# Attention scores in ten full banks instead of twelve partly filled ones

## The chip, the cores and the metric

One NeuronCore of a Trainium2 chip runs the whole kernel as one program. The metric is the device time of an execution in microseconds (us), the median of several. The engines are named as in the profile: PE is TensorE (PEld its weight loads), DVE is VectorE, ACT is ScalarE, POOL is GpSimd, and SP the queue that issues the loads. Each works through its own list of instructions strictly in the order of the program and waits at semaphores for the others.

## What is computed

One decoder layer on 512 tokens of width 1024, batch 1: a half-weighted SwiGLU, a mixer, a second half-weighted SwiGLU and a final RMS norm, each on a normalised input. The mixer projects the tokens once and has two head groups: four heads of gated linear attention (GLA) and eight heads of dilated attention, whose outputs are joined and projected by `w_out`. The part at issue is the dilated attention:

```python
q = rope_partial(aq...) * (ATT_HD ** -0.5)      # 8 heads of 64, rotary on the first 16 dims
k = rope_partial(ak...)
# for (window, dilation) in ((128, 1), (512, 4), (2048, 16)):
s = where(causal and in the window and on the stride, q @ k^T, -inf)
p = exp(s - max(s)); den = sum(p)
o = (p @ v) / den;  lse = max(s) + log(den)
# the three branches are mixed with softmax over their lse
o_att = rms_norm(sum(softmax(lse) * o), att_out_norm)
```

The kernel computes the three branches as one causal softmax with a mask in `const` that adds the log of the number of branches in which a key is seen.

## The kernel before

**Precision.** A weight product is made of three matmuls on rounded pairs (`product`, lines 1260 to 1262: high by high, high by low, low by high). So ACT rounds each weight unit from `raw` into `w_hi` (line 480, `split`) and DVE subtracts it into `w_lo` (line 776); PE waits for the count `w_split`. The matmuls of attention itself (lines 1566, 1582 and 1599) are full float32, each of those of 1566 and 1599 recorded as two instructions.

**Pairs, tiles, strips.** The eight heads are four pairs p; a pair fills the 128 partitions, with its heads e = 0 and 1 in the lower and upper 64. For a query tile i of 128 tokens the causal keys are 128(i+1) wide: a *strip* of 128, 256, 384 or 512 columns. A step s of the attention loop handles some strips of both heads in the banks `ps[4]` (e = 0) and `ps[5]` (e = 1), at most 512 columns each. Before, `ATT_TILES = ((0, 1), (2,), (3,))` gives each pair three steps of 384, 384 and 512 columns, so there are 12 steps.

**The stages of a step s**, each on its engine at loop index k:

- PE `scores(s)` at k = s (line 1566). The first step of a pair waits for `rope_done` of 2p+2 (query and key tile of the pair rotated), every step for `s_masked` of the step before.
- DVE `mask_scores(s)` at k = s (line 962): masks out of the bank into `probs` and takes the row maximum, one instruction for each strip and head.
- ACT `exp_scores(s)` at k = s (line 653): one exponential for each strip and head, with the row sum.
- DVE `scale_probs(s)` at k = s+1 (lines 984 and 991): reciprocal of the sums, then the scaling. In odd steps below `SHARED_FROM` ACT does both heads of the scaling (`scale_scalar`, line 672), from `SHARED_FROM` on ACT does e = 1 and DVE e = 0.
- PE `transpose_probs(s)` at k = s+2 (line 1582) into the banks 2 and 3, which ACT's `move_probsT(s)` copies out at k = s+2 (line 682).
- PE `weigh_values(s)` at k = s+3 (line 1599) adds to the bank 6 or 7 of the pair.

**What lies between.** PE fills each step with other work: first the projection of the remaining query and key tiles (`project_heads(n, w, half)`, half a tile of 12 products, at the indices `HEAD_STEPS`; two halves of the tile (1, 0) stand ahead of the loop), then the GLA part of the output projection (`gla_part(m, half)`, 6 products, at `PART_STEPS`). A projected tile is copied by ACT (`move_tile`, line 629, at `TILE_STEPS`) and rotated: DVE `rotate(n)` shuffles and multiplies by the sine (lines 942 and 945), POOL multiplies by the cosine (line 472), DVE `rotated(n)` adds the two (line 951) and counts `rope_done`. DVE also has `gla_gated_output` (line 1063) at k below 3, `low_concat` (line 1069), and the splits of weight units: `split_next(U + 10)` and `split_next(U + 11)` at k = 1 and 4. The unit U + 14 is split in quarters (`round_quarter` on ACT, line 662, k = 7 to 10; `split_quarter` on DVE, line 974, k = 8 to 11); only its last quarter raises `w_split`. When a pair is finished, ACT `high_heads(p)` (lines 690 and 691) and DVE `low_heads(p)` (line 997) take it out of its bank.

The order on PE in a step is this:

```python
for k in range(ATT_STEPS + 3):
    if k < ATT_STEPS:
        scores(k)
    # project_heads where HEAD_STEPS has k, gla_part where PART_STEPS has k
    if 2 <= k < ATT_STEPS + 2:
        transpose_probs(k - 2)
    if k >= 3:
        weigh_values(k - 3)
```

Of the kernel before, what the change touches and what calls it, by code (L numbers as in the profile page):

```python
# [32 lines left out]
P = 128  # L33
# [38 lines left out]
ATT_TILES = ((0, 1), (2,), (3,))  # L72
PER_PAIR = len(ATT_TILES)
ATT_STEPS = PER_PAIR * ATT_H // 2
# [3 lines left out]
SHARED_FROM = 8  # L78
# [3 lines left out]
TILE_STEPS = (0, 1, 2, 4, 5, 7)  # L82
HEAD_STEPS = (0, 0, 1, 1, 2, 3, 4, 4, 5, 6)
PART_STEPS = (7, 8, 10, 11, 12, 13, 13, 14)
# [6 lines left out]
def layer_program(nc, xw_dram, positions, gains_in, up1, down1, w_proj, w_ga, w_v, w_a2, w_o, up2, down2,  # L91
                  const_in, final_gain, out):
    ctx = ExitStack()
    with ctx:
# [67 lines left out]
        negm = sb("negm", [P, 4 * ATT_H], F32, mix)  # L162
        den = sb("den", [P, 4 * ATT_H], F32, mix)
        rden = sb("rden", [P, 4 * ATT_H], F32, mix)
# [184 lines left out]
        def strips(s):  # L349

            out, at = [], 0
            for i in ATT_TILES[s % PER_PAIR]:
                out.append((i, slice(at, at + P * (i + 1))))
                at += P * (i + 1)
            return out

        def strip_width(s):
            return strips(s)[-1][1].stop

        def stat(s, i, e):  # L360
            return 2 * (ST * (s // PER_PAIR) + i) + e

# [113 lines left out]
        def _(act):  # L476
# [170 lines left out]
            def exp_scores(s):  # L647
                for e in range(2):
                    act.wait_ge(s_masked, 2 * s + e + 1)
                    for i, cols in strips(s):  # L650
                        q = stat(s, i, e)
                        strip = probs[s % PROB_BUFS][e][:, cols]
                        ins = nc.scalar.activation(strip, strip, ACT.Exp, bias=negm[:, q:q + 1], scale=-1.0,
                                                   accum_out=den[:, q:q + 1])
                    ins.then_inc(exp_done, 1)
# [9 lines left out]
            def scale_scalar(s):  # L665
                act.wait_ge(rden_done, s + 1)
                for e in range(2):
                    if on_scalar(s, e):
                        for i, cols in strips(s):
                            q = stat(s, i, e)  # L670
                            strip = probs[s % PROB_BUFS][e][:, cols]
                            ins = nc.scalar.activation(strip, strip, ACT.Copy, scale=rden[:, q:q + 1])
                        ins.then_inc(act_scaled, 1)
# [14 lines left out]
            def high_heads(p):  # L688
                act.wait_ge(pv_done, PER_PAIR * (p + 1))
# [6 lines left out]
            for k in range(ATT_STEPS + 2):  # L696
                if k in TILE_STEPS:
                    tile = 2 + TILE_STEPS.index(k)
                    move_tile(tile // 2, tile % 2)
                if k == 8:  # L700
                    scale_scalar(k - 1)
                    move_probsT(k - 2)
                if k < ATT_STEPS:
                    exp_scores(k)
                if 1 <= k <= ATT_STEPS and k != 8 and on_scalar(k - 1, 1):
                    scale_scalar(k - 1)
                if k >= 2 and k != 8:
                    move_probsT(k - 2)
                if k in (1, 4):
                    n = (1, 4).index(k) + 1  # L710
                    split_next(U + 9 + n, 0, T + 19 + 2 * n)
                if 7 <= k < 11:
                    round_quarter(U + 14, k - 7, T + 25)
                if 1 <= k <= GLA_H:
                    high_concat(k - 1)
                if k in (7, 10, 12):
                    high_heads((7, 10, 12).index(k))
# [54 lines left out]
        def _(dve):  # L772
# [181 lines left out]
            def mask_scores(s):  # L954
                for e in range(2):
# [3 lines left out]
                    for i, cols in strips(s):  # L959
                        q = stat(s, i, e)  # L960
# [18 lines left out]
            def scale_probs(s):  # L979

                tiles = ATT_TILES[s % PER_PAIR]
                pair = slice(stat(s, tiles[0], 0), stat(s, tiles[-1], 1) + 1)
# [3 lines left out]
                for e in range(2):  # L986
                    if not on_scalar(s, e):
                        for i, cols in strips(s):
                            q = stat(s, i, e)
# [193 lines left out]
            for k in range(ATT_STEPS + 1):  # L1183
                rotates = k in TILE_STEPS
                if k == 8:
                    scale_probs(k - 1)
                if k < ATT_STEPS:
                    mask_scores(k)
                if k in (6, 8):
                    rotated(k - 1 if k == 8 else 6)  # L1190
                if k and k != 8:
                    scale_probs(k - 1)
                if rotates:
                    rotate(2 + TILE_STEPS.index(k))
                if k < 3:
                    gla_gated_output(k + 1)
                if rotates and k < 5:
                    rotated(2 + TILE_STEPS.index(k))
# [3 lines left out]
                if k in (1, 4):  # L1202
                    split_next(U + 10 + (1, 4).index(k), 0)
                if 8 <= k < 12:
                    split_quarter(U + 14, k - 8)
                if k in (8, 11, 12):
                    low_heads((8, 11, 12).index(k))
                if k == 12:
# [48 lines left out]
        def _(pe):  # L1257
# [291 lines left out]
            project_heads(1, 0, 0)  # L1549
            project_heads(1, 0, 1)  # L1550

            def scores(s):
                p = s // PER_PAIR
                if s % PER_PAIR == 0:
                    pe.wait_ge(rope_done, 2 * p + 2)
# [4 lines left out]
                for i, cols in strips(s):  # L1560
                    pieces = 2 if i else 1
                    width = P * (i + 1) // pieces
                    for c in range(pieces):
                        for e in range(2):
# [5 lines left out]
                            if i == strips(s)[-1][0] and c == pieces - 1:  # L1570
# [15 lines left out]
            def weigh_values(s):  # L1586
                p = s // PER_PAIR
                if s % PER_PAIR == 0:
# [6 lines left out]
                for i, cols in strips(s):  # L1595
# [45 lines left out]
            for k in range(ATT_STEPS + 3):  # L1641
                if k < ATT_STEPS:
                    scores(k)
                for h in range(len(HEAD_STEPS)):
                    if HEAD_STEPS[h] == k:
                        project_heads((h + 2) // 4 + 1, (h + 2) % 4 // 2, (h + 2) % 2)
# [140 lines left out]
```

## Time and profile before

| | before |
|---|---|
| median of 3 runs | 963.0 us (962.96 to 963.06) |
| the profiled execution: its own time | 962.81 us |
| its span, first to last instruction | 961.0 us |
| PE busy | 953.0 us of it |
| DVE busy, ACT busy, POOL busy | 491.4, 338.7, 52.3 us |
| granted TensorE clock, mean | 0.999 |
| attention loop on PE (first scores to the end of the last weighing) | 488.1 to 560.3 us of the span |

Times in rows are microseconds from the start of the span. In a timeline row the first number is the start and the second the duration; consecutive instructions of an engine overlap at their ends, so what an instruction costs its engine is the distance to the next start. In the chain of work that ended last, pieces stand end to end.

### The profile page before, as it was taken

The numbers are of one execution on the slowest core, as the hardware profiler recorded it, in microseconds if no ns is written. First come the engines' busy times: TensorE is split into PE (matmuls) and PEld (weight loads), VectorE is DVE, ScalarE is ACT, GpSimd is POOL, SyncE is SP. The second block draws the span as 40 slices with busy tenths as digits, with TensorE's granted clock in tenths as the row PEclk, the third lists the DMA queues.
The fourth block names the chain that finished last, engine by engine and source line by source line (L and its number), as shares of the span: only waits on it lengthen the run. The fifth ranks groups of instructions, "written<-read, shape, count | busy, mean of one in ns | idle before, by whom it ended". The sixth has DMA issues, their size and how long they took to land.

```text
span 961.0 us, 12088 instructions
## 1 busy us (share of the span) xinstructions
PE 953.0 (99%) x4714; PEld 776.2 (81%) x4714; DVE 491.4 (51%) x634; ACT 338.7 (35%) x440; POOL 52.3 (5%) x35
## 2 busy tenths in 40 slices
PE   9999999999999999999999999999999999999997
PEld 6888888888888887888778778788888888888885
DVE  6854443334443556554487768744443235644326
ACT  7323321122222334631446963433322122222313
POOL 0870000000000000000022000000000000000000
PEclk9999999999999999999999999999999999999999
DMA  8232222332221233222212012232222332255412
GB/s 324 87 132 87 76 77 92 110 127 88 91 111 55 83 102 128 88 89 88 89 44 89 29 61 87 91 129 87 87 77 87 99 131 88 90 151 152 110 44 88
DMA packets 33187, 94.76 MB, mean 99 GB/s; under 512 B 18560, under 2 KB 19840, under 8 KB 24960
## 3 DMA queue, kind: packets, MB, share of 16 engines
q1 hardware_dynamic: 16080, 91.89, 27.1%
q10 hardware_dynamic: 17072, 2.38, 1.6%
q8 instruction: 24, 0.39, 0.2%
q14 instruction: 11, 0.09, 0.0%
HBM read 90.07 MB, written 2.10 MB: 96 GB/s over the span
## 4 chain that ended last, share of the span: by engine, by line
PE 98%; DVE 1%; issue 1%; ACT 0%; DVEq 0%
PE bank L1260 31%; PE bank L1261 30%; PE bank L1262 30%; PE bank L1566 1%; PE bank L1599 1%; PE bank L1582 1%; PE bank L1378 1%; PE bank L1312 0%; PE bank L1320 0%; PE bank L1322 0%; PE bank L1277 0%; PE bank L1461 0%; DVE x_tok L1075 0%; PE bank L1498 0%; PE bank L1447 0%
## 5 line engine op out<-in xcount | busy, mean ns | idle before, releaser
L1260 PE MATMUL bank<-h_hi,w_hi 128*128 128x512 f32 x824 | 323.5, 393 | 0.0
L1262 PE MATMUL bank<-h_hi,w_lo 128*128 128x512 f32 x824 | 320.8, 389 | 0.0
L1261 PE MATMUL bank<-h_lo,w_hi 128*128 128x512 f32 x824 | 320.7, 389 | 0.0
L480 ACT ACTIVATE w_hi<-raw 128x2048 fp32r<-128x2048 f32 (+2 forms) x87 | 154.7, 1778 | 331.8 <-PE bank L1262 329.9
L776 DVE TENSOR_TENSOR w_lo<-raw,w_hi 128x2048 fp32r<-128x2048 f32 (+2 forms) x87 | 184.6, 2122 | 83.7 <-ACT w_hi L480 83.2
L1260 PEld LDWEIGHTS bank<-h_hi,w_hi 128*128 128x128 f32 x824 | 154.7, 188 | 36.4 <-issue 3.8
L1262 PEld LDWEIGHTS bank<-h_hi,w_lo 128*128 128x128 f32 x824 | 154.7, 188 | 32.3
L1261 PEld LDWEIGHTS bank<-h_lo,w_hi 128*128 128x128 f32 x824 | 154.7, 188 | 32.2 <-issue 0.7
L822 DVE TENSOR_TENSOR prod<-bank,rstd 128x512 f32<-128x512 f32 x44 | 30.4, 690 | 175.9 <-PE bank L1262 175.9
L1260 PE MATMUL bank<-g_hi,w_hi 128*128 128x512 f32 x272 | 105.8, 389 | 0.0
L1261 PE MATMUL bank<-g_lo,w_hi 128*128 128x512 f32 x272 | 105.8, 389 | 0.0
L1262 PE MATMUL bank<-g_hi,w_lo 128*128 128x512 f32 x272 | 105.8, 389 | 0.0
L521 ACT ACTIVATE gate<-gate 128x512 f32<-128x512 f32 x44 | 27.8, 632 | 158.4 <-DVE gate L820 158.3
L838 DVE SCALAR_TENSOR_TENSOR x<-bank,x 128x512 f32 (+1 forms) x24 | 16.6, 692 | 91.0 <-PE bank L1262 91.0
L1260 PEld LDWEIGHTS bank<-g_hi,w_hi 128*128 128x128 f32 x272 | 51.1, 188 | 10.6
L1261 PEld LDWEIGHTS bank<-g_lo,w_hi 128*128 128x128 f32 x272 | 51.1, 188 | 10.6
L1262 PEld LDWEIGHTS bank<-g_hi,w_lo 128*128 128x128 f32 x272 | 51.1, 188 | 10.6
L820 DVE TENSOR_TENSOR gate<-bank,rstd 128x512 f32<-128x512 f32 x44 | 30.2, 685 | 24.9 <-PE bank L1262 22.9
L472 POOL TENSOR_TENSOR projT<-projT,rope_c 128x512 f32<-128x512 f32 x8 | 13.9, 1733 | 455.0 <-DVE square L942 431.3
L831 DVE TENSOR_TENSOR g_lo<-prod,g_hi 128x512 f32 (+1 forms) x44 | 33.5, 760 | 0.7 <-ACT g_hi L525 0.7
L825 DVE TENSOR_TENSOR prod<-prod,gate 128x512 f32<-128x512 f32 x44 | 31.7, 722 | 3.2 <-ACT gate L521 0.6
L1260 PE MATMUL bank<-w_hi,g_hi 128*128 128x512 f32 x80 | 31.1, 389 | 0.0
(217 smaller groups left out, 841.5 us busy)
## 6 DMA issues: line engine op xcount, KB each, us to landing
raw<-in_up SPq DMA_DIRECT2D x43, 1024.0 KB, 4.8
raw<-in_w_proj SPq DMA_DIRECT2D x8, 1024.0 KB, 4.8
raw<-in_down1a SPq DMA_DIRECT2D x8, 768.0 KB, 4.4
raw<-in_down2a SPq DMA_DIRECT2D x8, 768.0 KB, 4.3
raw<-in_down1b SPq DMA_DIRECT2D x8, 640.0 KB, 3.8
raw<-in_down2b SPq DMA_DIRECT2D x5, 1024.0 KB, 4.9
raw<-in_w_v SPq DMA_DIRECT2D x4, 1024.0 KB, 4.8
raw<-in_w_o SPq DMA_DIRECT2D x4, 1024.0 KB, 4.8
```

Source lines behind the costliest of these rows:

```text
L472: nc.gpsimd.tensor_tensor(projT[:, t, :], projT[:, t, :], rope_c[:], ALU.mult).then_inc(rope_cos, 1)
L480: nc.scalar.activation(w_hi[u % 2][:, 0:size], raw[u % 2][:, 0:size], ACT.Copy).then_inc(w_round, 1)
L521: nc.scalar.activation(gate[:], gate[:], ACT.Silu).then_inc(silu_done, 1)
L776: nc.vector.tensor_tensor(w_lo[u % 2][:, 0:size], raw[u % 2][:, 0:size], w_hi[u % 2][:, 0:size].bitcast(F32), ALU.subtract).then_inc(w_spl ...
L820: nc.vector.tensor_tensor(gate[:], ps[bank][:], rstd[:], ALU.mult).then_inc(tile_out, 1)
L822: nc.vector.tensor_tensor(prod[:], ps[bank + 1][:], rstd[:], ALU.mult).then_inc(tile_out, 1)
L825: nc.vector.tensor_tensor(prod[:], prod[:], gate[:], ALU.mult).then_inc(g_mul, 1)
L831: nc.vector.tensor_tensor(g_lo[:, f, :], prod[:], g_hi[:, f, :].bitcast(F32), ALU.subtract).then_inc(g_ready, 1)
L838: nc.vector.scalar_tensor_tensor(x[:, m, 0:S], ps[4 + j][:], 0.5, x[:, m, 0:S], ALU.mult, ALU.add).then_inc(tile_out, 1)
L1260: nc.tensor.matmul(out, a_hi, b_hi, start=first, stop=False)
L1261: nc.tensor.matmul(out, a_hi, b_lo, start=False, stop=False)
L1262: return nc.tensor.matmul(out, a_lo, b_hi, start=False, stop=last)
```

## The change

The strips of two neighbouring pairs are packed together, so that each of ten steps has exactly 512 columns in each bank. For the pairs 0 and 1 (and again for 2 and 3) the five steps hold, as (pair, query tile): (0,0) with (0,2); (0,3); (0,1) with (1,1); (1,0) with (1,2); (1,3). The third of them holds a strip of either pair. `PAIR_BEGIN` is (0, 2, 5, 7) and `PAIR_END` (2, 4, 7, 9). The strips and their widths stay the same.

The work between the steps is placed anew: the second query/key tile of pair 1 is projected ahead of the loop (two more half tiles there, eight instead of ten in the loop), `SHARED_FROM` is 6, the split of U + 12 comes at k = 0 and that of U + 13 at k = 3, the quarters at k = 6 to 9 on ACT and 7 to 10 on DVE, and `gla_part`, `high_heads` and `low_heads` at earlier indices. The order on ACT that was special at k = 8 is gone.

```diff
 N_CONST = 1795
-ATT_TILES = ((0, 1), (2,), (3,))
-PER_PAIR = len(ATT_TILES)
-ATT_STEPS = PER_PAIR * ATT_H // 2
+ATT_TILES = tuple(tuple((base + p, i) for p, i in tiles) for base in (0, 2)
+                  for tiles in (((0, 0), (0, 2)), ((0, 3),), ((0, 1), (1, 1)), ((1, 0), (1, 2)), ((1, 3),)))
+ATT_STEPS = len(ATT_TILES)
+PAIR_BEGIN = [min(s for s in range(ATT_STEPS) if any(q == p for q, i in ATT_TILES[s])) for p in range(4)]
+PAIR_END = [max(s for s in range(ATT_STEPS) if any(q == p for q, i in ATT_TILES[s])) for p in range(4)]
 HALF = S // 2
...
 MOVES = 16
-SHARED_FROM = 8
+SHARED_FROM = 6
 NORM = {0: 0, 2: 3}
...
 ATT_BANKS = (6, 2, 3, 7)
-TILE_STEPS = (0, 1, 2, 4, 5, 7)
-HEAD_STEPS = (0, 0, 1, 1, 2, 3, 4, 4, 5, 6)
-PART_STEPS = (7, 8, 10, 11, 12, 13, 13, 14)
+TILE_STEPS = (0, 0, 1, 3, 4, 6)
+ROTATE_STEPS = (0, 1, 2, 3, 4, 6)
+HEAD_STEPS = (0, 0, 1, 2, 3, 3, 4, 5)
+PART_STEPS = (6, 7, 8, 9, 10, 11, 11, 12)
 MAGIC = 1.5 * 2.0 ** 23
...
             out, at = [], 0
-            for i in ATT_TILES[s % PER_PAIR]:
-                out.append((i, slice(at, at + P * (i + 1))))
+            for p, i in ATT_TILES[s]:
+                out.append((p, i, slice(at, at + P * (i + 1))))
                 at += P * (i + 1)
...
         def strip_width(s):
-            return strips(s)[-1][1].stop
-
-        def stat(s, i, e):
-            return 2 * (ST * (s // PER_PAIR) + i) + e
+            return strips(s)[-1][2].stop
+
+        def stat(s, p, i, e):
+
+            return 4 * s + 2 * ATT_TILES[s].index((p, i)) + e
...
             def high_heads(p):
-                act.wait_ge(pv_done, PER_PAIR * (p + 1))
+                act.wait_ge(pv_done, PAIR_END[p] + 1)
                 nc.scalar.activation(sq_att[p], ps[6 + p % 2][:], ACT.Square).then_inc(att_squared, 1)
...
             for k in range(ATT_STEPS + 2):
-                if k in TILE_STEPS:
-                    tile = 2 + TILE_STEPS.index(k)
-                    move_tile(tile // 2, tile % 2)
-                if k == 8:
-                    scale_scalar(k - 1)
-                    move_probsT(k - 2)
+                for tile in range(2, 8):
+                    if TILE_STEPS[tile - 2] == k:
+                        move_tile(tile // 2, tile % 2)
                 if k < ATT_STEPS:
                     exp_scores(k)
-                if 1 <= k <= ATT_STEPS and k != 8 and on_scalar(k - 1, 1):
+                if 1 <= k <= ATT_STEPS and on_scalar(k - 1, 1):
                     scale_scalar(k - 1)
-                if k >= 2 and k != 8:
+                if k >= 2:
                     move_probsT(k - 2)
-                if k in (1, 4):
-                    n = (1, 4).index(k) + 1
+                if k in (0, 3):
+                    n = (0, 3).index(k) + 1
                     split_next(U + 9 + n, 0, T + 19 + 2 * n)
-                if 7 <= k < 11:
-                    round_quarter(U + 14, k - 7, T + 25)
+                if 6 <= k < 10:
+                    round_quarter(U + 14, k - 6, T + 25)
                 if 1 <= k <= GLA_H:
                     high_concat(k - 1)
-                if k in (7, 10, 12):
-                    high_heads((7, 10, 12).index(k))
+                if k in (6, 8, 11):
+                    high_heads((6, 8, 11).index(k))
             nc.scalar.activation(credit[:], ones[:, 0:1], ACT.Ln)
...
             for k in range(ATT_STEPS + 1):
-                rotates = k in TILE_STEPS
-                if k == 8:
-                    scale_probs(k - 1)
                 if k < ATT_STEPS:
                     mask_scores(k)
-                if k in (6, 8):
-                    rotated(k - 1 if k == 8 else 6)
-                if k and k != 8:
+                if k == 5:
+                    rotated(6)
+                if k:
                     scale_probs(k - 1)
-                if rotates:
-                    rotate(2 + TILE_STEPS.index(k))
+                if k in ROTATE_STEPS:
+                    rotate(2 + ROTATE_STEPS.index(k))
                 if k < 3:
                     gla_gated_output(k + 1)
-                if rotates and k < 5:
-                    rotated(2 + TILE_STEPS.index(k))
+                if k in ROTATE_STEPS and k != 4:
+                    rotated(2 + ROTATE_STEPS.index(k))
                 if 2 <= k < 2 + GLA_H:
...
                     low_concat(g, cat_lo[:, g, :], o_gla[g][:], cat_hi[:, g, :])
-                if k in (1, 4):
-                    split_next(U + 10 + (1, 4).index(k), 0)
-                if 8 <= k < 12:
-                    split_quarter(U + 14, k - 8)
-                if k in (8, 11, 12):
-                    low_heads((8, 11, 12).index(k))
-                if k == 12:
+                if k in (0, 3):
+                    split_next(U + 10 + (0, 3).index(k), 0)
+                if 7 <= k < 11:
+                    split_quarter(U + 14, k - 7)
+                if k in (7, 9, 10):
+                    low_heads((7, 9, 10).index(k))
+                if k == ATT_STEPS:
                     add_heads(1)
...
             gla_spread()
-            project_heads(1, 0, 0)
-            project_heads(1, 0, 1)
+            for part_of in range(4):
+                project_heads(1, part_of // 2, part_of % 2)
             def scores(s):
-                p = s // PER_PAIR
-                if s % PER_PAIR == 0:
-                    pe.wait_ge(rope_done, 2 * p + 2)
+                if s in PAIR_BEGIN:
+                    pe.wait_ge(rope_done, 2 * PAIR_BEGIN.index(s) + 2)
                 if s:
...
                     pe.wait_ge(gla_half, 2)
-                for i, cols in strips(s):
+                for p, i, cols in strips(s):
                     pieces = 2 if i else 1
...
             def weigh_values(s):
-                p = s // PER_PAIR
-                if s % PER_PAIR == 0:
+                if s in PAIR_BEGIN:
+                    p = PAIR_BEGIN.index(s)
                     if p >= 2:
...
                 pe.wait_ge(pt_out, 2 * s + 2)
-                for i, cols in strips(s):
+                for p, i, cols in strips(s):
                     for j in range(i + 1):
...
                     if HEAD_STEPS[h] == k:
-                        project_heads((h + 2) // 4 + 1, (h + 2) % 4 // 2, (h + 2) % 2)
+                        project_heads(h // 4 + 2, h % 4 // 2, h % 2)
                 for h in range(len(PART_STEPS)):
...
                         gla_part(h // 2, h % 2)
```

## Rows read from the trace of the kernel before

**Rows 1.** The page: busy time, granted clock (tenths), chain that ended last.

```profile
PE 953.0 (99%) x4714; PEld 776.2 (81%) x4714; DVE 491.4 (51%) x634; ACT 338.7 (35%) x440; POOL 52.3 (5%) x35
...
PEclk9999999999999999999999999999999999999999
...
PE 98%; DVE 1%; issue 1%; ACT 0%; DVEq 0%
```

**Rows 2.** The chain in order of time, 486 to 566: start, us, what.

```profile
488.14 0.87 PE bank L1566 x12
489.01 0.43 PE bank L1260
...
494.67 0.85 PE bank L1566 x8
...
517.65 0.87 PE bank L1582 x8
518.52 0.81 PE bank L1599 x12
519.33 1.06 PE bank L1566 x8
...
524.02 1.02 PE bank L1599 x16
...
560.28 0.43 PE bank L1260
...
563.31 0.86 PE bank L1660 x2
```

**Rows 3.** Timeline of DVE in the attention loop.

```profile
488.29 2.29 DVE L776 TENSOR_TENSOR w_lo<-raw,w_hi 128x2048 fp32r<-128x2048 f32 x1
490.49 0.28 DVE L962 CUSTOM_DVE_ANT_0 probs<-bank,const 128x128 f32<-128x128 f32 x1
...
491.61 0.73 DVE L942 STREAM_SHUFFLE square<-projT 128x512 f32<-128x512 f32 x1
...
492.99 1.79 DVE L1063 SCALAR_TENSOR_TENSOR gt<-gt,gains,projT 128x512 f32<-128x512 f32 x1
494.70 0.68 DVE L951 TENSOR_TENSOR projT<-projT,square 128x512 f32<-128x512 f32 x1
...
496.73 1.01 DVE L991 TENSOR_SCALAR probs<-probs,rden 128x128 f32<-128x128 f32 x4
...
503.55 0.68 DVE L962 CUSTOM_DVE_ANT_0 probs<-bank,const 128x512 f32<-128x512 f32 x1
...
504.77 0.15 DVE L984 RECIPROCAL rden<-den 128x2 f32<-128x2 f32 x1
...
513.67 0.74 DVE L942 STREAM_SHUFFLE sumsq<-projT 128x512 f32<-128x512 f32 x1
...
516.40 0.69 DVE L951 TENSOR_TENSOR projT<-projT,sumsq 128x512 f32<-128x512 f32 x1 [1.26 <-POOL projT L472]
```

**Rows 4.** Timeline of POOL: one of the eight cosine products.

```profile
492.49 1.74 POOL L472 TENSOR_TENSOR projT<-projT,rope_c 128x512 f32<-128x512 f32 x1 [6.17 <-DVE square L942]
```

**Rows 5.** Timeline of ACT in the attention loop.

```profile
514.64 1.49 ACT L672 ACTIVATE probs<-probs,rden 128x128 f32<-128x128 f32 x4
...
540.71 0.42 ACT L653 ACTIVATE probs<-probs,negm 128x128 f32<-128x128 f32 x1
...
542.47 0.73 ACT L672 ACTIVATE probs<-probs,rden 128x512 f32<-128x512 f32 x1
...
546.23 1.09 ACT L682 ACTIVATE probsT<-bank 128x512 f32<-128x512 f32 x2
547.19 0.65 ACT L662 ACTIVATE w_hi<-raw 128x512 fp32r<-128x512 f32 x1
...
548.75 0.75 ACT L653 ACTIVATE probs<-probs,negm 128x512 f32<-128x512 f32 x1
```

**Rows 6.** Timeline of PE at the start of the program.

```profile
1.49 5.49 PE L1378 MATMUL bank<-rope_c 128*128 128x512 f32 x6 [1.49 <-DVE rope_c L876]
```

More of the change, by code:

```diff
@@ L161, in layer_program @@
         gt.append([sb(f"gt2_{p}", [P, S], F32, mix) for p in range(2)])
-        negm = sb("negm", [P, 4 * ATT_H], F32, mix)
-        den = sb("den", [P, 4 * ATT_H], F32, mix)
-        rden = sb("rden", [P, 4 * ATT_H], F32, mix)
+        negm = sb("negm", [P, 4 * ATT_STEPS], F32, mix)
+        den = sb("den", [P, 4 * ATT_STEPS], F32, mix)
+        rden = sb("rden", [P, 4 * ATT_STEPS], F32, mix)
         late = ExitStack()
@@ L649, in exp_scores @@
                     act.wait_ge(s_masked, 2 * s + e + 1)
-                    for i, cols in strips(s):
-                        q = stat(s, i, e)
+                    for p, i, cols in strips(s):
+                        q = stat(s, p, i, e)
                         strip = probs[s % PROB_BUFS][e][:, cols]
@@ L668, in scale_scalar @@
                     if on_scalar(s, e):
-                        for i, cols in strips(s):
-                            q = stat(s, i, e)
+                        for p, i, cols in strips(s):
+                            q = stat(s, p, i, e)
                             strip = probs[s % PROB_BUFS][e][:, cols]
@@ L958, in mask_scores @@
                         dve.wait_ge(pt_done, 2 * (s - PROB_BUFS) + e + 1)
-                    for i, cols in strips(s):
-                        q = stat(s, i, e)
+                    for p, i, cols in strips(s):
+                        q = stat(s, p, i, e)
                         ins = nc.vector.tensor_tensor_reduce(
@@ L979, in scale_probs @@
             def scale_probs(s):
-                tiles = ATT_TILES[s % PER_PAIR]
-                pair = slice(stat(s, tiles[0], 0), stat(s, tiles[-1], 1) + 1)
+                pair = slice(4 * s, 4 * s + 2 * len(ATT_TILES[s]))
                 dve.wait_ge(exp_done, 2 * s + 2)
@@ L987, in scale_probs @@
                     if not on_scalar(s, e):
-                        for i, cols in strips(s):
-                            q = stat(s, i, e)
+                        for p, i, cols in strips(s):
+                            q = stat(s, p, i, e)
                             strip = probs[s % PROB_BUFS][e][:, cols]
@@ L1559, in scores @@
                     pe.wait_ge(gla_half, 2)
-                for i, cols in strips(s):
+                for p, i, cols in strips(s):
                     pieces = 2 if i else 1
@@ L1569, in scores @@
                                                     start=True, stop=True)
-                            if i == strips(s)[-1][0] and c == pieces - 1:
+                            if (p, i) == strips(s)[-1][0:2] and c == pieces - 1:
                                 last.then_inc(s_done, 1)
@@ L1594, in weigh_values @@
                 pe.wait_ge(pt_out, 2 * s + 2)
-                for i, cols in strips(s):
+                for p, i, cols in strips(s):
                     for j in range(i + 1):
```

## The prediction

> **What bounds the kernel.** I read the page first. PE is busy for 99% of the span, and the chain that ended last is PE for 98% [rows 1]; DVE and ACT have about half and a third of the span, but these are averages over stages that differ. So a change pays only if it takes time off PE's own list, and it costs if it makes PE wait. Next I read that chain in order of time through the attention loop [rows 2]. The pieces stand end to end from 488.1 to 560.3 us, and nothing but PE's lines is in them: before the change PE waits here for practically nobody. Last I read the timelines of DVE, POOL and ACT in the same stretch [rows 3, 4, 5], because the question becomes when they are due. The granted clock is full in all 40 slices [rows 1].
>
> **What PE saves.** The strips and their widths are the same, so the matmuls, transposes and weighings are the same in number and shape. What falls away is the fixed part of a block. Sixteen weighings take 1.02 and twelve 0.81 [rows 2], so one is 0.0525 and 0.18 a block is fixed. A score block of eight instructions of 256 columns takes 1.06; at 0.0525 for 128 columns its columns are 0.84 and 0.22 is fixed, and twelve of 128 columns at 0.87 say the same [rows 2]. The first product after such a block takes 0.43, while 24 products with that first one take 5.66 from 489.01 to 494.67 [rows 2]: 0.227 each and 0.20 for the return. Two blocks fewer of each kind save 2 x 0.22 + 2 x 0.18 = 0.8. Score blocks followed by products plus weighings that go straight to products were 15 and are 14, which is 0.2. The twelve transposing blocks of the chain have about 0.5 more in them than 80 transposes at the rate of the eight that take 0.87 [rows 2]; that is short waits and one block that comes right after scores. I give the change all of it. The saving is 1.5 us, 0.16% of the time. ACT saves four copies' fixed parts and DVE two reciprocals, which is worth nothing by itself as PE is the bound.
>
> **What a step of the new loop costs PE.** Every step has 1.06 of scores, then its filler (half a tile: 2.93 with the return; half a `gla_part`: 1.57), from k = 2 on 0.87 of transposes and from k = 3 on 1.02 of weighing. A full step with `gla_part` is 4.52. Against this I walk through DVE's and ACT's lists in their new order and ask at each wait of PE who is late. At most of them PE is later. At three it isn't.
>
> **First wait: step 2, for the rotation of pair 1.** The third step holds a strip of pair 1, so its scores wait for `rope_done` of 4; before, this was asked for at the fourth step, in the middle of a long list. On PE the extra 24 products ahead of the loop (24 x 0.227 = 5.5) put `scores(0)` at 493.6 to 494.7. Two half tiles (5.66), `scores(1)` (1.06) and one half tile (2.93) follow, so PE is at `scores(2)` at 504.3. DVE sits idle until 494.7, as `mask_scores(0)` is first in its list, and then has, up to the end of `rotated(3)`: the mask of step 0, 1.39 (1.12 for 128 and 256 columns twice, from 490.49 to 491.61, and 0.27 for the wider strips); rotation with the gated output, 3.09 (491.61 to 494.70), as the line 1063 takes 1.79 while the cosine product of POOL runs; `rotated(2)`, 0.60; the weight split now at k = 0, 2.20 (488.29 to 490.49); the mask of step 1, 1.22 (503.55 to 504.77); reciprocal 0.20; the scaling of step 0, 1.07 (four at 128 and 256 are 0.93, and two are wider by 128); rotation and gated output again, 3.09; and `rotated(3)`, 0.68 [rows 3, 4]. The sum is 13.5, so the pair is ready at 508.2. With 0.1 for the signal PE waits 4.0 us. The split's own input, ACT's rounding, comes from its list at about 499.4, in time. Bounds: 4.2 if everything on DVE shows its own duration without overlap of ends; 3.1 if POOL didn't slow line 1063 at all (1.79 against 0.68 for a plain neighbour would save 1.1 twice, but the addition waits for POOL's 1.74 anyway, which leaves about 0.45 each time). I take 4.0, as the sequence is the same as in the rows. Queued behind this wait are the half tile of step 2 and the first transposes. Nobody else is late by it, since DVE and ACT are then ahead of PE.
>
> In steps 3 to 5 PE doesn't wait: step 3 has two half tiles (8.6 us), the weight split of U + 13 delays the mask of step 4 to 526.8, and PE wants it at 527.7. That 0.9 is the smallest slack there.
>
> **Second wait: step 7, for the rotation of pair 3.** It needs `rope_done` of 8, and `rotate(7)` is at k = 6 on DVE, behind the mask of step 6 and the reciprocal of step 5. Counted from PE's start of step 6: scores 1.06, mask 1.22, reciprocal 0.20, and rotation through POOL 3.42 (513.67 to 516.40, and 0.69) [rows 3]; with the signal 6.0. PE arrives after 4.52. It waits 1.5. Bounds: 1.2 to 1.7, as this chain doesn't depend on how late anybody was before.
>
> **Third wait: step 10, for the last quarter of U + 14.** `gla_part(2, 0)` stood at k = 12 and stands at k = 10, and is now the first thing of a step that has no scores. It needs `w_split`, so `split_quarter(3)` (DVE, k = 10) behind `round_quarter(3)` (ACT, the last thing of k = 9). From PE's start of step 9, with ACT free: scores 1.06, mask of head 0 0.7, two exponentials of 512 columns 1.4, scaling of 128 and 384 columns 0.8, the copies of the transposes 0.96, the rounding 0.65 [rows 5], the subtraction 0.7 like every DVE instruction of that width [rows 3]: 6.3 against 4.52, so 1.8 at the least. ACT isn't free. Its list at k = 8 has four exponentials 2.0 (1.76 for 128 and 256 columns twice, from 540.71 to 542.47, wider by 0.24), scaling 0.8, copies 0.96, and a quarter and `high_heads(1)` 1.56 (547.19 to 548.75) [rows 5]: 5.3 against PE's 4.52. So it begins step 9 0.9 late, and the wait is 2.7. The lag from k = 6 (another `high_heads` and 1.6 for scaling both heads, 1.49 with narrower strips [rows 5]) has been absorbed by the second wait. If the second wait isn't there, that lag of about 1.5 comes through here instead, so the sum of the two is steadier than either. Bounds 1.8 to 4.2.
>
> Behind step 12, `low_heads(2)`, two additions and two `add_gla` now stand close before `low_heads(3)` on DVE, all 0.7 each. They were done by the time of the last weighing and now end just after PE wants them: 0.2 us. The rest follows PE as before.
>
> **The sum.** -1.5 + 4.0 + 1.5 + 2.7 + 0.2 = +6.9 us. On the profiled execution (962.8) that is 969.7; the median of before is 0.2 above that execution, so 969.9.
>
> **The clock.** Inside its work PE has no idle time of that length before. At the start of the program, where it had done nothing, six float32 matmuls of 512 columns took 5.49 with the tail of the last, 0.8 to 0.9 each, where two of the same width take 0.86 together later, 0.43 each [rows 2, 6]. That is the lower of the levels, 1.2 against 2.4 GHz, and it cost those six about 2 us. Whether the wait of 4.0 brings it back is not in the rows. The Trainium skill ("TensorE: Matmul & The Clock Gate", Part 1) states that the clock goes back to 1.2 GHz after the array has been idle for a stretch. By that rule the sum could be +8.9, by the rows alone, which show no fall, +6.9. I leave it out of the sum, since this idle time is short and stands alone.
>
> **Rivals.** *Nothing is late* (forecast on the other side): the walk is wrong for DVE in steps 0 and 1, it keeps PE's 9.65 instead of 13.5, and the later waits are hidden likewise. Then only the saving is left: 961.5. It decides at step 2; for it speaks that PE never waits here before, against it that DVE's rows in that very sequence leave no room of 3.9. Chance 0.06. *Saving and one small wait cancel* (the first wait below 2): 963, no change. The other two would have to be hidden as well. Chance 0.04. *Only part of the waits*: the first alone gives 963.0 - 1.5 + 4.0 = 965.5, the first and second 967.0 (963.0 - 1.5 + 5.5). What speaks for it is that ACT's lag was worked out from many terms. Chance 0.13. *All three*, 968.5 to 971.5: 0.60. *All three and the clock falls* after the first: the slow stretch costs about 2 us as at the start, partly taken back where PE would have waited anyway: 971 to 973.5. What speaks for it is that the wait is long beside anything in the trace before; against it, that it stands alone and is followed by dense work. Chance 0.17.
>
> **How the numbers follow.** The time is that of all three waits, 969.9. The range leaves out the first two rivals and the half of the third in which only one wait shows, and ends within the clock's case: 966.7 to 972.6. A difference of 0.2%, 1.9 us, is about what this kernel's measurement tells from none. Faster 0.06, same 0.04, slower 0.90, since even the first wait alone exceeds 0.2%.
>
> **What will show it.** In the profile after, the waits of PE should have `scores` (now about L1566) behind line 951's addition twice, about 4.0 and 1.5 us, and a product behind the quarter's subtraction, about 2.7. The loop should end 6.6 us later than 560.3 in the chain, the score blocks should all be 1.06, and the granted clock should stay at 2.4 GHz. The forecast is wrong if DVE's list of steps 0 and 1 is shorter than PE's, if ACT reaches the last quarter earlier, or if the clock falls.

## The result, and the profile after

The changed kernel takes 973.17 us (median of 5 runs, 971.7 to 974.53), the kernel before 962.96 (962.68 to 963.06). The ratio is 1.0109, with a 95% interval of 1.0099 to 1.012: 10.2 us slower. I forecast 969.9 with a range of 966.7 to 972.6, so the direction and two thirds of the size were right and the median lies 0.6 us outside. The profiled execution took 972.18 us, with a span of 970.4 and a mean granted clock of 0.996.

The waits of PE in the profile after (who waited for whom: us in total, times, the longest). Before, the list had only the last of these waits, with 1.5 as well (there as L1378 behind L876; the line numbers have moved):

```profile
PE bank L1562 <- DVE projT L952: 5.3, 2, 3.9
PE bank L1257 <- DVE w_lo L975: 2.7, 1, 2.7
PE bank L1375 <- DVE rope_c L877: 1.5, 1, 1.5
```

L1562 is a score matmul, L952 the addition of `rotated`, L975 the subtraction of `split_quarter`: the three waits of the prediction with 3.9, 1.4 and 2.7 us, where it had 4.0, 1.5 and 2.7. The next rows are DVE's list in front of the first wait (timeline of DVE, after); they answer to [rows 3]:

```profile
495.00 0.29 DVE L963 CUSTOM_DVE_ANT_0 probs<-bank,const 128x128 f32<-128x128 f32 x1 [4.11 <-PE bank L1562]
...
497.76 1.79 DVE L1063 SCALAR_TENSOR_TENSOR gt<-gt,gains,projT 128x512 f32<-128x512 f32 x1
499.48 0.68 DVE L952 TENSOR_TENSOR projT<-projT,square 128x512 f32<-128x512 f32 x1
500.08 2.28 DVE L777 TENSOR_TENSOR w_lo<-raw,w_hi 128x2048 fp32r<-128x2048 f32 x1
502.28 0.68 DVE L963 CUSTOM_DVE_ANT_0 probs<-bank,const 128x512 f32<-128x512 f32 x1
...
504.76 0.71 DVE L943 STREAM_SHUFFLE sumsq<-projT 128x512 f32<-128x512 f32 x1
...
506.12 1.75 DVE L1063 SCALAR_TENSOR_TENSOR gt<-gt,gains,projT 128x512 f32<-128x512 f32 x1
507.80 0.68 DVE L952 TENSOR_TENSOR projT<-projT,sumsq 128x512 f32<-128x512 f32 x1
```

DVE idles for 4.1 us, then runs from 495.0 to 508.5 without waiting for PE: 13.5 us, the sum of the prediction. What the prediction left out of its sum stands in the chain in order of time (after), behind that wait:

```profile
507.80 0.69 DVE projT L952
508.53 1.35 PE bank L1562 x16
509.89 0.72 PE bank L1257
510.61 0.43 PE bank L1258
511.04 0.43 PE bank L1259
...
512.75 0.30 PE bank L1257
513.05 0.23 PE bank L1258
```

The scores take 1.35, where the same block behind the same wait takes 1.16 at full clock (e5 below), and the products behind them are 0.43 apart, and 0.23 again from 513 on. The stages of the same profile (busy time of each engine, and PEclk) say why:

```profile
504.00:509.00 5.00, 1.15 (x12) 0.69 (x12) 4.44 (x8) 1.04 (x3) 1.70 (x1) 1.00 0.44 184
509.00:512.00 3.00, 3.00 (x19) 2.39 (x16) 2.04 (x11) 1.27 (x5) 0.00 (x0) 0.56 0.03 8
512.00:515.00 3.00, 3.00 (x16) 2.35 (x15) 2.96 (x4) 2.34 (x7) 1.74 (x1) 0.87 0.00 0
```

From 509 to 512 us the granted clock is 0.56 (most of it the lower level, 1.2 GHz), and PE comes out of 3.9 us of idle. Scores and products up to the first transposes, 508.53 to 514.22, take 5.69; in e5, at full clock, they take 4.11 (508.57 to 512.68). That is 1.6 us lost. So the loop, from the first scores at 493.90 to the end of the last weighing at 569.05, takes 75.15 us. Without waits its blocks are 64.9 (10 x 1.06, 10 x 0.87, 10 x 1.02, 144 products at 0.2275 and 13 returns of 0.20). Of the other 10.3 the waits are 8.0, the clock is 1.6, and 0.7 is scattered over starts behind waits and products of 0.24.

This profile is one of the faster executions. The three slower ones have a lower mean clock, 0.992 to 0.994, so more lies in the clock there than it shows.

### The profile page after: what moved, and what is told of

It is laid out like the page before. It is cut to its first block, busy times and chain, and to the rows that moved or that the text cites. A ratio compares the mean times of both kernels' runs of the same rounds, so it can differ in the third digit from the quotient of the medians.

```text
span 970.4 us, 12070 instructions
## 1 busy us (share of the span) xinstructions
PE 954.4 (98%) x4714; PEld 777.8 (80%) x4714; DVE 490.6 (51%) x631; ACT 339.1 (35%) x437; POOL 52.3 (5%) x35
## 4 chain that ended last, share of the span: by engine, by line
PE 95%; DVE 2%; ACT 1%; issue 1%; POOLq 0%; DVEq 0%
PE bank L1257 30%; PE bank L1258 29%; PE bank L1259 29%; PE bank L1562 1%; PE bank L1595 1%; PE bank L1578 1%; PE bank L1375 1%; PE bank L1309 0%; PE bank L1319 0%; PE bank L1317 0%; DVE probs L963 0%; ACT probs L657 0%; PE bank L1274 0%; DVE gt L1063 0%; DVE w_lo L777 0%
## 5 line engine op out<-in xcount | busy, mean ns | idle before, releaser
L1259 PEld LDWEIGHTS bank<-h_hi,w_lo 128*128 128x128 f32 x824 | 155.0, 188 | 32.5
```

The lines of the kernel that those rows point to most:

```text
L1259: return nc.tensor.matmul(out, a_lo, b_hi, start=False, stop=last)
```

## The experiments

Each was timed beside the kernel before on the same chip, with four or five executions, eleven for e8 to e10. e1 to e4 ran on one chip (median of before 962.84), e5 to e10 on another (962.63, for e9 and e10 962.58); where I compare across the two, 0.2 of the difference is the chip's.

**e1: the changed kernel again.**

> The changed kernel once more, unaltered, for a second profile and more times. If the fall of the clock behind the wait at step 2 is what lies between my 969.9 and the 973.2 measured, then the times must spread over some 3 us again (971.5 to 974.5), the slower executions must have the lower mean clock (0.992 to 0.996), and the second profile must show a stretch of half clock behind the wait of step 2 and perhaps one at the wait of step 10. The rival, that something constant was left out of my sum, expects the same excess in each execution and no relation to the clock.

Measured: 973.92 us, from 971.35 to 974.9. With the five runs of the result there are nine executions, each with its mean clock. At 0.996: 971.35, 971.7, 972.18. At 0.994: 973.17, 974.48. At 0.993 and 0.992: 973.78, 974.05, 974.53, 974.9. The kernel before has 0.998 to 0.999 there and a spread of less than 0.7. The second profile, of an execution at 0.992, in the same stages and one more:

```profile
504.00:509.00 5.00, 1.14 (x11) 1.05 (x12) 3.87 (x6) 0.46 (x1) 1.70 (x1) 0.76 0.42 170
509.00:512.00 3.00, 3.00 (x15) 2.39 (x14) 1.89 (x11) 1.12 (x5) 0.00 (x0) 0.50 0.01 3
512.00:515.00 3.00, 3.00 (x15) 2.43 (x14) 2.96 (x4) 2.18 (x6) 1.74 (x1) 0.76 0.00 0
...
555.00:560.00 5.00, 2.33 (x18) 1.79 (x15) 1.80 (x4) 3.21 (x8) 0.00 (x0) 0.78 0.16 20
560.00:565.00 5.00, 5.00 (x36) 3.96 (x35) 0.00 (x0) 1.08 (x2) 0.00 (x0) 0.88 0.47 193
```

Here the clock is down longer behind the first wait, and it falls a second time behind the third one, of 2.7 us. The waits themselves are the same, 3.9, 1.4 and 2.7. So the same program with the same waits loses a varying amount to the clock. In the result's profile the lower level runs from 509.4 to 512.8, so it begins 0.8 after PE had resumed; here it runs from 506.6, inside the wait, to 513.4, and again from 557.9 to 561.3. The loop takes 77.4 us here, where it took 75.15 there.

**e2: PE kept busy in the first wait.**

```diff
             for k in range(ATT_STEPS + 3):
+                if k == 2:
+                    pe.wait_ge(tile_out, BANK_CREDIT + T + 17)
+                    for _ in range(4):
+                        nc.tensor.matmul(ps[2][:], ident, const[:, C_TRI:C_TRI + S], start=True, stop=True)
                 if k < ATT_STEPS:
                     scores(k)
```

> Four full float32 matmuls of 512 columns on constants, into bank 2 which is free there, ahead of the wait of scores(2): 3.4 us of work that nobody needs, inside an idle time of 3.9. Nothing else is changed. Clock theory: scores(2) starts at the same time as before, the products behind it take 0.23 and not 0.43, so 1.7 us less than the profile of the change and 2 to 3 us less than its median, 970 to 971, the mean clock 0.998 or more, and the spread of the times shrinks to under 1 us. Rival (the excess has another cause): 973.2, no gain, or a loss if the extra matmuls delay scores(2).

Measured: 971.66 us, 971.12 to 971.81, mean clock 0.996 (0.998 expected): 2.3 less than e1 beside it, and a spread of 0.7. More matmuls make the kernel faster. It is 0.7 above the clock theory's 970 to 971, as the mean clock isn't back: behind the third wait it still falls; the profile has 1.00 from 504 to 515 us and 0.66 from 555 to 560.

**e3: the weight split back at k = 1.**

```diff
-                if k in (0, 3):
-                    split_next(U + 10 + (0, 3).index(k), 0)
+                if k in (1, 3):
+                    split_next(U + 10 + (1, 3).index(k), 0)
```

> Only the weight split of U+12 on DVE goes back from k = 0 to k = 1, as it stood before the change. Theory A (my sum of durations, read as if each term could be taken out): the wait of 3.9 loses 2.2, is 1.7, and the clock may stay up, so 968 to 970. Theory B: without the split DVE reaches mask_scores(1) at once when scores(1) is done (501.7 in the profile of the change, where it began at 502.3), and from there mask 1.2, reciprocal 0.2, scaling 1.1 and rotation 3.8 still end at 508.0; so only 0.5 us of the wait goes, it is 3.4, and the time is 972.5 with the clock falling as before.

Measured: 973.31 us (970.96 to 974.41), 0.8 above the time of theory B, but its wait: PE's longest wait for L952 is 3.4 instead of 3.9. The timeline of DVE:

```profile
501.59 0.69 DVE L963 CUSTOM_DVE_ANT_0 probs<-bank,const 128x512 f32<-128x512 f32 x1 [1.61 <-PE bank L1562]
...
507.13 0.68 DVE L952 TENSOR_TENSOR projT<-projT,sumsq 128x512 f32<-128x512 f32 x1
507.73 2.28 DVE L777 TENSOR_TENSOR w_lo<-raw,w_hi 128x2048 fp32r<-128x2048 f32 x1
```

Without the split DVE only gets its own idle time, 1.6 us, ahead of `mask_scores(1)`. A term of 2.2 in a sum was worth 0.5 when taken out, because the mask can't begin before its scores. The cause of the first wait is that a rotation stands behind a mask that waits for PE, while PE then waits for the rotation.

**e4: rotations out from between the masks** (first wait gone).

```diff
+            rotate(2)
+            gla_gated_output(1)
+            rotated(2)
             for k in range(ATT_STEPS + 1):
                 if k < ATT_STEPS:
                     mask_scores(k)
+                if k == 0:
+                    rotate(3)
+                    gla_gated_output(2)
+                    rotated(3)
...
-                if k in ROTATE_STEPS:
+                if k > 1 and k in ROTATE_STEPS:
                     rotate(2 + ROTATE_STEPS.index(k))
-                if k < 3:
+                if k == 2:
                     gla_gated_output(k + 1)
-                if k in ROTATE_STEPS and k != 4:
+                if k > 1 and k in ROTATE_STEPS and k != 4:
```

> The rotations are taken out from between the masks: tile 2 is rotated ahead of mask_scores(0), in the 4 us in which DVE was idle, and tile 3 right behind mask_scores(0), each with its gated output; the splitting stays where the change has it. By the walk pair 1 is ready at 500.2 and mask_scores(1) at 503.6, before PE asks at 504.7: no wait at step 2. Clock theory: 3.9 for the wait and 1.7 to 2.7 for the slow stretch go, 966.6 to 967.6, mean clock 0.998 or more. Rival without the clock: 969.3. Rival that DVE is late elsewhere then: a new wait in steps 3 to 5, over 968.

Measured: 968.17 us (967.68 to 969.06), mean clock 0.995 to 0.997, 5.8 less than e1. The first wait is gone from the list of PE's waits, and no other took its place in steps 3 to 5:

```profile
PE bank L1264 <- DVE w_lo L975: 2.7, 1, 2.7
...
PE bank L1569 <- DVE projT L952: 1.4, 1, 1.4
```

3.9 of the 5.8 is the wait, and the remaining 1.9 I put down to the clock behind it. It is 0.6 above the expectation (and just over the 968 of the rival whose new wait isn't there), which had allowed for no fall of the clock behind the third wait; the profile has 0.85 and 0.80 there, in the stages 550 to 555 and 555 to 560.

**e5: PE kept busy in the first and the third wait.** As e2, and ahead of the work of step 10:

```diff
+                if k == ATT_STEPS:
+                    pe.wait_ge(s_masked, 2 * ATT_STEPS)
+                    for _ in range(3):
+                        nc.tensor.matmul(ps[4][:], ident, const[:, C_TRI:C_TRI + S], start=True, stop=True)
```

> The idle time of PE is filled with matmuls that nobody needs at both long waits: four ahead of scores(2) as in e2, and three ahead of the product that waits at step 10 for the last quarter of U+14 (into bank 4, which the scores of the last step have left). All waits of the change stay. Clock theory: the profiles of e1, e2 and e3 show half clock behind either wait, for 3.4 or 6.8 us; with both filled the clock stays up, the mean clock is that of the kernel before, the spread of the times is as small as there (under 1 us) and the time is the sum of my prediction without the clock, 962.8 - 1.5 + 3.9 + 1.5 + 2.7 + 0.2 = 969.6, 0.3 either way. Rival (something besides waits and clock is in the 973): it stays above 970.5.

Measured: 970.33 us, 970.01 to 970.65, and a mean clock of 0.999 in each of the five executions. The kernel does all that the changed one does and seven matmuls more that nobody reads, and it takes 3.6 us less than e1. Its real work starts as late behind either wait. The timeline of PE shows the scores of step 2 at 508.57 (508.53 in the result's profile), and the added matmuls of L1645 in the third wait, with the product behind them 0.05 after the subtraction that it needs, which ends at 556.39:

```profile
508.57 1.16 PE L1562 MATMUL bank<-projT 64*128 64x128 f32 x16 [0.43 <-DVE projT L952]
...
553.69 2.84 PE L1645 MATMUL bank<-const 128*128 128x512 f32 x6
556.44 0.50 PE L1257 MATMUL bank<-cat_hi,w_hi 128*128 128x512 f32 x1
```

The stages of its profile:

```profile
509.00:512.00 3.00, 3.00 (x24) 2.50 (x21) 2.19 (x11) 1.43 (x6) 0.00 (x0) 1.00 0.03 8
512.00:515.00 3.00, 3.00 (x25) 2.40 (x25) 2.96 (x4) 3.00 (x9) 1.72 (x1) 1.00 0.00 0
...
555.00:560.00 5.00, 5.00 (x35) 3.29 (x33) 0.69 (x1) 2.36 (x5) 0.00 (x0) 1.00 0.43 156
560.00:565.00 5.00, 5.00 (x37) 4.07 (x38) 0.00 (x0) 1.54 (x4) 0.00 (x0) 1.00 0.15 57
```

The time lies 0.4 above my range and 0.2 under the bound of the rival, so by itself it decides little; the clock and the profiles do. Against the kernel before beside it e5 is 970.33 - 962.63 = 7.7 slower, the result 10.2 and e1 11.1: the clock's part of the change is 2.5 to 3.4 us. In the profiles the loop takes 73.6 us in e5, so the clock took 1.6 in the result's profile and 3.8 in e1's. The 7.7 stands against the +6.9 of my sum.

**e6: the second wait gone.** `rotate(7)` on DVE ahead of the mask of step 6:

```diff
+                if k == 6:
+                    rotate(7)
                 if k < ATT_STEPS:
                     mask_scores(k)
...
-                if k in ROTATE_STEPS:
+                if k != 6 and k in ROTATE_STEPS:
                     rotate(2 + ROTATE_STEPS.index(k))
```

> The rotation of the last tile goes ahead of the mask of step 6 on DVE (rotate(7), then mask_scores(6), then rotated(7)), so that pair 3 is ready at 539.6 and PE, asking at 540.1, doesn't wait at step 7. Theory A (waits add up): 1.4 less than the change, 971.8. Theory B (my prediction's remark that the sum of the second and third wait is steadier than either): ACT's list from step 6 on ends later by 0.3 since its exponentials begin later, the last quarter of U+14 is due at the same moment or 0.3 later, and PE only waits longer for it: 4.1 to 4.4 at step 10 instead of 2.7, the time as before, 973 to 974.5.

Measured: 974.13 us (973.75 to 974.46), theory B. The list of PE's waits in its profile:

```profile
PE bank L1259 <- DVE w_lo L975: 4.0, 1, 4.0
PE bank L1564 <- DVE projT L952: 3.9, 1, 3.9
```

The second wait is gone and the third has grown from 2.7 to 4.0, 0.1 less than theory B has. The clock doesn't hide a gain here: e1 and e6 have two falls each in their profiles, 10.2 us at the lower level in both, and both loops take 77.4 us. The last quarter of U + 14 comes at the end of ACT's list, and that list is what ends it, whether PE waits once or twice on the way.

**e7: the third wait gone.** The quarters one step earlier, on ACT at k = 5 to 8 and on DVE at k = 6 to 9:

```diff
-                if 6 <= k < 10:
-                    round_quarter(U + 14, k - 6, T + 25)
+                if 5 <= k < 9:
+                    round_quarter(U + 14, k - 5, T + 25)
...
-                if 7 <= k < 11:
-                    split_quarter(U + 14, k - 7)
+                if 6 <= k < 10:
+                    split_quarter(U + 14, k - 6)
```

> The four quarters of U+14 are rounded and split one step earlier (k = 5 to 8 on ACT, 6 to 9 on DVE). Step 5 has room for one on ACT. By the walk the last quarter is split before PE asks for it at 555.2, and no other wait takes its place: the transposes of step 10 need ACT's copies of step 9 at about 556, they are asked for at 556.8. So 2.7 us of wait and, in part of the executions, the 1 to 2 us of half clock behind it go: 969.3 to 970.5 with the clock still falling behind the first wait. Rival: ACT is the bound through steps 6 to 9, and the wait only moves to transposes or weighing in step 10, over 971.5.

Measured: 969.1 us (968.65 to 970.0), 4.8 less than e1 (4.6 with each against the kernel before beside it), a little below the expected interval. The list of waits keeps the first two and nothing else in the loop:

```profile
PE bank L1562 <- DVE projT L952: 5.3, 2, 3.9
```

2.7 of the gain is the wait: the profile, with one fall of the clock as in the result's, has a loop of 72.4 us instead of 75.15. The rest I put down to the second fall, which some executions of the change have.

**e8: all three gone.** e4, e6 and e7 together, and

```diff
-            return s % 2 == 1 if s < SHARED_FROM else e == 1
+            return s % 2 == 1 if s < SHARED_FROM else e == 1 and s != 8
```

> The three moves of e4, e6 and e7 together, and the scaling of step 8 goes to DVE for both heads, as ACT would otherwise be late by 0.7 at step 10. If the ten full banks save what I worked out (fixed parts of blocks, 1.5 us) and nothing else is late, 961.3, that is 0.16% faster than the kernel before, with its clock and its small spread. If the saving is not there, 962.8; if ACT is late in steps 7 to 10 after all, 962 to 963.5, with waits of transposes for L676 or L686 in the profile.

Measured: 962.82 us (961.87 to 963.24, 11 runs) against 962.63: ratio 1.0003, interval 0.9994 to 1.0012. That is no change, and 1.5 above what I expected. By the time alone the saving might be missing or ACT late, the two other cases of the expectation; the profile speaks for small waits. Its profile's loop goes from 493.18 to 559.38, 66.2 us, where before the same work takes 488.14 to 560.28 less 5.46 for the two half tiles that now stand ahead of it, 66.7 [rows 2]. So the ten full banks save 0.5 in the loop, not 1.5. Three small waits stand where I had none:

```profile
532.82 1.09 PE L1604 MATMUL bank<-probsT,x 128*64 128x128 f32 x16
534.15 1.16 PE L1571 MATMUL bank<-projT 64*128 64x128 f32 x16 [0.24 <-DVE projT L952]
...
541.56 1.11 PE L1587 MATMUL bank<-const,probs 128*128 128x128 f32 x8
...
549.76 1.10 PE L1587 MATMUL bank<-const,probs 128*128 128x128 f32 x8
```

The score block of step 7 starts 4.9 after that of step 6 instead of 4.5. The transposes at k = 8 and at k = 10 cost some 0.4 and 0.2 more in all; their blocks are 1.11 and 1.10 long instead of 1.03. That is 0.9 to 1.0. And 0.6 is lost behind the loop, which is the same code: from the end of the last weighing to the sums of the second FFN (L1277 before, L1283 here) it is 44.7 us before (560.28 to 604.98) and 45.3 in e8 (559.38 to 604.71). About 0.1 is `low_heads(3)`, the wait that I had put at 0.2. The other 0.5 comes evenly: the first 138 matmuls from the attention sums on take 32.52 us instead of 31.99, and from there on the two run alike. Every profile of a changed kernel, the result's as well, has 32.5 there, so it isn't from the edits of e8.

**e9: first and third gone, the second left.** The edits of e4 and e7.

> e4 and e7 together: the first and the third wait are taken away, the second, at step 7 for the rotation of pair 3, stays. In e6 its removal alone gained nothing, because ACT's lag came out at step 10 instead. Here nothing waits for ACT at step 10, so the second wait should have its own price: against e8, which has all three gone, 1.4 us more for the wait and up to 0.4 less as ACT and DVE catch up in it (e8's profile shows 0.2 at the same scores and 0.2 to 0.4 at two transposes): 963.7 to 964.3. With an idle time of 1.4 at most the clock stays up (none of the profiles shows a fall behind the second wait). Rival (the second wait is hidden by something and free, as e6 seemed to say): 962.8.

Measured: 963.71 us (963.49 to 964.01, 11 runs), ratio 1.0012 (1.0003 to 1.0021), clock 0.999. The list of PE's waits:

```profile
PE bank L1569 <- DVE projT L952: 1.4, 1, 1.4
```

The second wait is 1.4 as ever and costs 0.9 net against e8, where in e6 its removal gained nothing. It is worth something only when nothing behind it waits for ACT.

**e10: e8 with less for ACT in step 6.** `SHARED_FROM = 5`, and on DVE:

```diff
-                if k == 5:
-                    rotated(6)
+                if k in (5, 6):
+                    rotated(k + 1)
...
-                if k > 1 and k in ROTATE_STEPS and k != 4:
+                if k > 1 and k in ROTATE_STEPS and k not in (4, 6):
                     rotated(2 + ROTATE_STEPS.index(k))
```

> e8 with ACT's load in step 6 made smaller: scaling is shared from step 5 on (DVE takes head 0 of step 5, 0.8 less on ACT), and rotated(7) goes ahead of that scaling on DVE. In e8's profile step 7 starts 0.3 late and the transposes of steps 8 and 9 0.2 to 0.4, together 0.9 us, and I put all of it down to ACT's lag from step 6 and the rotation. If so, this version is 0.4 to 0.9 faster than e8: 962.0 to 962.4, just under the kernel before. Rival (the small waits come from DVE's masks or from issue): 962.8 as e8. Either way the difference to the kernel before is within 0.1%.

Measured: 962.16 us (961.66 to 962.47, 11 runs), 0.66 less than e8; against the kernel before the ratio is 0.9994, with an interval of 0.9985 to 1.0003. The timeline of PE in its profile, the last weighing before the scores of step 7, these scores, and the transposes at k = 8, 9 and 10:

```profile
533.18 1.09 PE L1604 MATMUL bank<-probsT,x 128*64 128x128 f32 x16
534.41 1.16 PE L1571 MATMUL bank<-projT 64*128 64x128 f32 x16
...
541.55 1.03 PE L1587 MATMUL bank<-const,probs 128*128 128x128 f32 x8
...
546.11 1.04 PE L1587 MATMUL bank<-const,probs 128*128 128x128 f32 x8
...
549.60 1.03 PE L1587 MATMUL bank<-const,probs 128*128 128x128 f32 x8
```

The transposes have their plain length, 1.03 to 1.04. The scores of step 7 gained only 0.1: they start 1.23 after the weighing, 1.33 in e8, where 1.02 is plain. The loop takes 65.6 us (493.54 to 559.13), 1.1 less than the 66.7 of before, and 0.6 of that is lost again behind the loop, as in e8. So the packing into ten full banks, with the three waits taken out, is worth 0.4 us, which this measurement doesn't tell from nothing.

## Why the prediction was right or wrong

**The three waits** were right in place, cause and size: 4.0, 1.5 and 2.7 forecast, 3.9, 1.4 and 2.7 in both profiles of the changed kernel. (ACT's lag in the third was 5.3 - 4.52 = 0.8 by its own terms, not 0.9, which would have made 2.6.) e4, e6 and e7 each remove one by moving exactly the work that the prediction named as late. The remark that the second and third wait together are steadier than either was right too (e6 against e9).

**The clock** is the step that failed. The prediction named its fall as a rival with a chance of 0.17 and a price of 2 us, and left it out of the sum, "since this idle time is short and stands alone". It fell in both profiles of the changed kernel, behind a wait of 3.9 us, and in e1 behind one of 2.7 as well, which I hadn't considered. With PE kept busy the spread shrinks to 0.6, and 2.5 to 3.4 us go with it (e5). Of the 10.2 measured, 7.7 is there without the clock and 2.5 is the clock; the forecast of 6.9 was short by that 2.5 and by 0.8 more. The page of the Trainium skill that I cited ("TensorE: Matmul & The Clock Gate", Part 1) was the better guide: by its rule the sum was +8.9, nearer to the +10.2 than mine without it. The prediction's argument that nothing in the rows showed a fall was no evidence, for inside its work the trace before has no idle time of that kind in which it could have shown. And at its end it does show a fall, which I overlooked: the last product ends at 954.5, PE does nothing more, and from 959.3 on the granted clock is at the lower level, too little to show in the tenths of the page. The last matmul of the timeline before and two stages of the same profile:

```profile
954.11 0.39 PE L1262 MATMUL bank<-w_hi,g_lo 128*128 128x512 f32 x1
...
959.00:960.00 1.00, 0.00 (x0) 0.00 (x0) 0.00 (x0) 0.00 (x0) 0.00 (x0) 0.63 1.05 365
960.00:961.00 1.00, 0.00 (x0) 0.00 (x0) 0.00 (x0) 0.00 (x0) 0.00 (x0) 0.50 0.01 2
```

The price of 2 us came from the durations of the first six matmuls, for which the view of the stages has 1.00, and it was of one fall; there were up to two, the first is longer in some executions, and in two profiles they cost 1.6 and 3.8.

**The saving of 1.5** was too large. In the loop 1.5 was expected and 0.5 came in e8; 0.9 to 1.0 went to small waits, of which e10 takes back 0.6, so that 1.1 of the 1.5 is there. The strips are the same, so ACT and DVE have nearly the same work in a loop that PE wants to finish sooner, and the saving of PE turned into waits for them. That is how I read e8 and e10 together; which of e10's two edits did it wasn't tried apart. The score blocks in the chain after are 1.06 to 1.07 each where nobody waits, as forecast, but for those of sixteen instructions, which take 1.09 (e8 and e10).

**The last 0.2** measured 0.1. **What no term had**: 0.5 us behind the loop, in the distance of the products. e5 shows the account at full clock: +6.9 forecast, +7.7 measured, of which 0.5 is this. The remaining 0.3 isn't told apart from the saving that was put too high.

**Open.** Why the same products behind the loop stand 0.4 us per hundred further apart after the change isn't settled; the code there is the same, and no wait stands in the profile. And why the clock falls behind the wait of 2.7 in some executions only is not shown by any run here, only that it does.

## What to carry to other kernels

When an engine that works without a gap is given waits, count the waits and then count what its clock does behind them: here three waits of 8 us together cost 10 to 11, and idle matmuls in them gave about 3 back. Walk through the lists of the other engines in their new order and compare arrival times at each wait; a term taken out of a late engine's sum is worth only what lies behind the last thing that this engine itself waits for (2.2 us of work, 0.5 us of time in e3). And before one of several waits is removed, ask which list ends the last of them: taking away the 1.4 us wait gained nothing until the one behind it was gone.

## What the runs showed of the hardware that I had not expected

The granted clock fell to the lower level in or just behind waits of 3.9, 3.4 and 2.7 us (profiles of e1, e3 and e2), within a kernel that is dense before and after, but behind the wait of 2.7 us not in each execution; behind the wait of 1.4 us no profile shows a fall. Matmuls on constants whose result nobody reads held it up (0.999 in each execution of e5). And the distance of identical 512-column products without any wait was not constant: 138 matmuls behind the attention sums took 31.99 us before and 32.52 in e8 and in the others with the change, with no wait in the profile and at full clock.
